# Expert stage: the down weights loaded from ScalarE's queue, gate and up weights left on SyncE's

## The reference, cut to what matters

```python
hn = rms_norm(h)                                  # 1040 x 1024
expert_idx, weights = top 2 of 8 experts in the best of 8 groups     # 64 experts
for every token t and each of its two experts e:
    g = hn[t] @ w_gate[e]                         # 1024 x 256
    u = hn[t] @ w_up[e]                           # 1024 x 256
    y = (silu(g) * u) @ w_down[e]                 # 256 x 1024
out[t] = h[t] + sum of weights * y
```

## Time and profile before

| | |
|---|---|
| time, median of 3 runs | 4101.42 us (4097.24 to 4104.04) |
| the profiled execution | 4109.06 us, span 4107.2 us |
| expert stage in the profile | 3415.4 us (first constant issued) to 4030.6 us (last scatter issued) |
| its assignment part | 3415.4 to 3473.7 us (first gate product) |
| its loop over the blocks | 3473.7 to 4030.6 us |
| loads of weights | 210 of 1024 KB, all on SyncE's queue |
| DMA queues over the span | q1 (SyncE's) 465.09 MB, q10 (ScalarE's) 112.70 MB, q0 (GpSimd's) 17.08 MB |

### The profile page before, as it was taken

The page is one execution under the profiler, slowest core; times in us unless marked ns, Lnnn a source line. Parts: engine busy times, 40 slices in busy tenths (PEclk is TensorE's granted clock), DMA queues, the critical chain, the costliest instruction groups (busy, mean ns, idle before and its releaser), DMA issues. The chain is left out here.

```text
span 4107.2 us, 80665 instructions
## 1 busy us (share of the span) xinstructions
PE 3411.6 (83%) x33244; PEld 2848.2 (69%) x33244; DVE 1585.4 (39%) x2597; ACT 995.8 (24%) x1970; POOL 345.2 (8%) x395
## 2 busy tenths in 40 slices
PE   7989988888859859998996799999959864978772
PEld 5867777788748759997986588888849643544441
DVE  3145643434245541115654345555444314111113
ACT  2022311122222021113443245444411011211111
POOL 0000000000000000000000223222100000222221
PEclk9999999999979979999998799999869965989986
DMA  3335455211344333324442311110033236999995
GB/s 103 95 101 190 148 180 182 88 49 43 113 148 139 125 94 93 93 74 151 162 142 92 97 27 52 48 38 23 23 108 119 87 95 248 414 417 409 410 410 197
DMA packets 325011, 598.26 MB, mean 146 GB/s; under 512 B 57427, under 2 KB 222140, under 8 KB 304728
## 3 DMA queue, kind: packets, MB, share of 16 engines
q1 hardware_dynamic: 275419, 465.09, 32.3%
q10 hardware_dynamic: 38436, 112.70, 7.8%
q0 software_dynamic: 10928, 17.08, 1.1%
HBM read 475.58 MB, written 139.97 MB: 150 GB/s over the span
## 5 line engine op out<-in xcount | busy, mean ns | idle before, releaser
L3052 PE MATMUL ex_bank_ps<-ex_w_gate_up_sb,ex_xT_sb 128*64 128x256 f32 x2240 | 290.9, 420 | 91.6 <-DMA ex_w_gate_up_sb<-in_w_up_e 89.9
L361 PE MATMUL in_bank_ps<-in_h_hi_sb,in_w_hi_sb 128*128 128x352 f32 (+4 forms) x968 | 332.6, 344 | 10.7 <-DVE in_w_lo_sb L316 10.7
L361 PE MATMUL in_bank_ps<-in_h_hi_sb,in_w_lo_sb 128*128 128x352 f32 (+4 forms) x968 | 332.6, 344 | 0.0
L361 PE MATMUL in_bank_ps<-in_h_lo_sb,in_w_hi_sb 128*128 128x352 f32 (+4 forms) x968 | 332.2, 343 | 0.0
L3052 PEld LDWEIGHTS ex_bank_ps<-ex_w_gate_up_sb,ex_xT_sb 128*64 128x64 f32 x2240 | 176.9, 152 | 214.6 <-issue 139.6
L1417 PE MATMUL mix_bank_ps<-mix_y_hi_sb,mix_wb_hi_sb 128*128 128x512 f32 (+2 forms) x480 | 171.5, 357 | 76.2 <-DVE mix_y_lo_sb L1498 54.0
L433 PE MATMUL qkv_tile_bank_ps<-in_h_hi_sb,qkv_tile_w_hi_sb 128*128 128x352 f32 (+1 forms) x576 | 188.9, 328 | 11.9 <-DVE qkv_tile_w_lo_sb L420 11.9
L361 PEld LDWEIGHTS in_bank_ps<-in_h_hi_sb,in_w_hi_sb 128*128 128x128 f32 (+1 forms) x968 | 181.2, 187 | 24.7 <-issue 11.4
L3240 DVE TENSOR_TENSOR ex_hidden_sb<-ex_silu_g_sb,ex_bank_ps 128x128 f32<-128x128 f32 x70 | 20.1, 288 | 453.3 <-ACT ex_silu_g_sb L3104 453.3
L361 PEld LDWEIGHTS in_bank_ps<-in_h_lo_sb,in_w_hi_sb 128*128 128x128 f32 (+1 forms) x968 | 181.3, 187 | 14.7
L361 PEld LDWEIGHTS in_bank_ps<-in_h_hi_sb,in_w_lo_sb 128*128 128x128 f32 (+1 forms) x968 | 181.3, 187 | 13.2
(11 more groups left out here) (460 smaller groups left out, 7714.4 us busy)
## 6 DMA issues: line engine op xcount, KB each, us to landing
ex_w_gate_up_sb<-in_w_gate_e SPq DMA_DIRECT2D x70, 1024.0 KB, 16.8
ex_w_gate_up_sb<-in_w_up_e SPq DMA_DIRECT2D x70, 1024.0 KB, 24.7
ex_w_down_sb<-in_w_down_e SPq DMA_DIRECT2D x70, 1024.0 KB, 25.0
in_w_sb<-in_w_in SPq DMA_DIRECT2D x45, 512.0 KB, 4.4
scr_p2T<-in_o_sb ACTq DMA_DIRECT2D x28, 520.0 KB, 3.0
qkv_x_sb<-scr_p2T SPq DMA_DIRECT2D x8, 1560.0 KB, 7.1
scr_p2T<-qkv_tile_o_sb ACTq DMA_DIRECT2D x24, 520.0 KB, 3.0
prep_tile_w_sb<-in_w_in SPq DMA_DIRECT2D x24, 512.0 KB
```

What stands on the lines that cost most here:

```text
L361: last = pe.matmul(bank[:width, 4 * s + n, 0:m], w_[:, s, k, 0:width], h_[:, k, a:a + m], start=(k == 0 and z == 0), stop=(k == KT - 1 and ...
L3052: last = t.matmul(bank[m * BT:(m + 1) * BT, GU_B + b % 2, 0:2 * P], xT[:, s, k, at:at + BT], wgu[:, ws, :, k, m * P:(m + 1) * P], start=(k ...
```

## The change

The down weights are loaded by ScalarE. Its first six loads stand ahead of its first wait, and each later pair of down loads stands behind the copies of the pair that frees the slots. SyncE issues gate and up alone and no longer waits for `y_done`. The last turn of ScalarE's loop is taken out of the loop, since there is nothing left to load behind it. No amount of data and no slot is changed.

```diff
@@ block.sync
-            def load_down(e, ws):
-                sp.dma_start(wd[:, ws, :, :],
-                             wd_d[ds(e, 1), :, :].rearrange("a (m p) d -> (a p) m d", m=M)).then_inc(d_ld[ws], 16)
-
             for b in range(TURN):
                 load_gate_up(b, b)
-                load_down(b, b)
             load_pairs(sp)
...
                 sp.wait_ge(gu_done, done(i, b))
                 load_gate_up(e, b % WS)
-
-                sp.wait_ge(y_done, done(i, b))
-                load_down(e, b % WS)
@@ block.scalar
             a.sem_inc(y_rdy, 2)
             c = Steps(a, ac)
+            def load_down(e, ws):
+                a.dma_start(wd[:, ws, :, :],
+                            wd_d[ds(e, 1), :, :].rearrange("a (m p) d -> (a p) m d", m=M)).then_inc(d_ld[ws], 16)
+
+            for b in range(TURN):
+                load_down(b, b)
             a.wait_ge(dv, at["shifted"])
...
             load_pairs(a)
-            with a.Fori(0, N_BLK // TURN) as i:
+            def compute(i, q):
...
+            with a.Fori(0, N_BLK // TURN - 1) as i:
                 for q in range(PT):
                     with in_use(a, i, q):
+                        compute(i, q)
+                    with in_use(a, i + 1, q):
                         for b in (2 * q, 2 * q + 1):
+                            load_down(a.value_load(table[0:1, ds((i + 1) * TURN + b, 1)], min_val=0, max_val=N_EXP - 1), b % WS)
+            for q in range(PT):
+                with in_use(a, N_BLK // TURN - 1, q):
+                    compute(N_BLK // TURN - 1, q)
```

More of the change, by code:

```diff
@@ L3095, in _ @@
             load_pairs(a)
-            with a.Fori(0, N_BLK // TURN) as i:
+            def compute(i, q):
+                for b in (2 * q, 2 * q + 1):
+                    s = b % 2
+                    a.wait_ge(gu_done, done(i, b, WS))
+                    a.wait_ge(h_rdy, done(i, b))
+                    a.activation(sg[:, s, :], bank[:, GU_B + s, 0:P], ACT.Silu).then_inc(sg_rdy, 1)
+                for b in (2 * q, 2 * q + 1):
+                    s = b % 2
+                    a.wait_ge(y_done, done(i, b, WS))
+                    a.wait_ge(y_free, done(i, b))
+                    a.activation(y[:, s, :], bank[:, Y_B + s, :], ACT.Copy).then_inc(y_rdy, 1)
+            with a.Fori(0, N_BLK // TURN - 1) as i:
                 for q in range(PT):
                     with in_use(a, i, q):
+                        compute(i, q)
+                    with in_use(a, i + 1, q):
                         for b in (2 * q, 2 * q + 1):
[L3100 to L3110, removed]
+                            load_down(a.value_load(table[0:1, ds((i + 1) * TURN + b, 1)], min_val=0, max_val=N_EXP - 1), b % WS)
+            for q in range(PT):
+                with in_use(a, N_BLK // TURN - 1, q):
+                    compute(N_BLK // TURN - 1, q)
         @block.vector
```

## The result

The changed kernel takes 4120.25 us (median of 5 runs, 4115.11 to 4124.24), the kernel before 4101.42 us: 1.0047 times as long, with a 95% interval of 1.0032 to 1.0061. Run again it was 1.0050 [1.0035, 1.0065], with medians of 4120.46 against 4104.22 us. By these ratios it is 19 to 20 us slower (by the medians 18.8 and 16.2); I had forecast +7.9 us.

A forecast was written before the change was run, and what follows sets the result against it. The prediction took transfers to bound the loop, and the constants' path to decide before it. Its terms, 8 − 0.7 − 1.9 + 2.5 = +7.9 us on 4101.4, gave 4109.3 us, with a range from 4099 to 4118.

The forecast's parts named there:

- GpSimd's rows: Gathers and scatters in the loop: a third queue costs each 1.3 us, covered by 4.9 us to spare a pair; cost 0.
- Six down loads beside the constants: Before the loop: constants take turns with ScalarE's first six down loads and land later, +8 us, between 0 and +12.3.
- First gather: Before the loop: the first weights start landing earlier, so the first gather may gain, −0.7 us, between 0 and −1.
- Start of the loop: First 10.2 us of loop loads: two blocks' gate and up are queued early and the transfer hole closes, −1.9 us.
- The long middle: The loop's 64 blocks: same bytes with the DMA engines full, so 0 us.
- the end: Behind the last loads: gate and up of block 69 become the last bytes, +2.5 us, between 0 and 2.7.
- ScalarE's own work: ScalarE in the loop: register loads and issues take some 2.6 us a pair, covered by 9.2 us; cost 0.
- A: Rival on the whole kernel: the constants slip through and there is no effect, −0.1 us, 4101.3 us; chance 0.16.
- B: Rival at the constants: engines serve whole loads in turn, so 12.3 us in place of 8, 4113.6 us; chance 0.13.
- C: Rival in the loop: ScalarE's down issues are held up and Silu comes late, +28 to +100 us, 4137 us; chance 0.08.
- D: Rival at the loop's end: two queues spread the rest evenly and constants slip through, −8.2 us, 4093.2 us; chance 0.06.

The follow-up runs named there:

- e1: The changed kernel, with ScalarE waiting for the seven constants before its first six down loads; 4109.79 us, 1.0015 of the kernel before.
- e2: The kernel before, with only its first six down loads moved to ScalarE's queue and all later ones on SyncE's; 4114.32 us, +0.29%.
- g1: The changed kernel, with GpSimd issuing the gather three pairs ahead behind its scatters, before their landing, and not waiting for that gather at once; 4117.91 us, 1.0042.
- g2: The changed kernel with both the constants waited for before ScalarE's first down loads and g1's early gather; 4106.28 us, 0.11% over the kernel before.
- h1: The changed kernel with w_down laid out for 8 KB rows on the down queue, gate and up products taking every second column; loop 570.6 us.
- g4: The changed kernel with each down load cut into two of half the columns, so rows are 2 KB instead of 4; loop 586.5 us.
- e3: The changed kernel, with GpSimd issuing the gather three pairs ahead behind its scatters, then waiting for that gather before going on; 4114.73 us, 1.0031.

## Why the prediction was wrong

The median, 4120.25 us, lies above the range, which ended at 4118, and the loss is more than twice the forecast's. The step that failed is that of GpSimd's rows, costed at 0: it cost 3 to 3.6 us of the 6 to 7 that the loop lost. The constants' term was right in kind and too small. Term by term:

*Six down loads beside the constants: +8 forecast, 10.4 measured* at the first reduce (15.2 behind the first constant against 4.8), 9 to 10 over the start, and 12 to 13 us in the times of e1 and e2. The mechanism, turns by packet, was right from 3418 us on: 367 packets against 365, and the row lengths move the price. The term was mis-sized. I had given the constants' own work 3.1 us on top of the turns as the upper end, and with 2 KB rows, where the turns cost half as much (4.1 us), 7.2 us are measured. So 2.2 us on top of the turns are there with 4 KB rows and 3.1 with 2 KB. With 8 KB rows 51 turns would take 16.4 us, more than the 15.3 us of all six loads, and 15.7 are measured, so nothing can be read there. The 2.5 us from 3413.5 to 3416 in which the constants' queue all but stood still are of this size; that they are the same time is argued. The forecast had no such gap.

*First gather: −0.7 forecast.* From the first reduce to the first gate product it is 53.1 us against 53.6 before, −0.4.

*Start of the loop: −1.9 forecast.* The share of the first ten us rose from 0.81 to 0.90 and not to 1.0: some −0.9 us of transfer.

*GpSimd's rows: cost 0 forecast.* This step failed. I took 8 turns of 0.159 us, 1.3 us for a gather or a scatter, against 4.9 us to spare. Measured: scatters +3.6 to 3.9 us, gathers +1.2 to +1.6 (8.1 before, 9.3 to 9.7 in e1, by the stretch). Three things were wrong in it. I held the 1.3 against the slack one at a time, where GpSimd's program puts gather, scatters and their landing in series. The scatters stand behind the gather on one queue: 24 rows an engine and not 8, and 24 x 0.159 = 3.8 us would fit; that is an estimate, and with one queue the scatters right behind a gather landed only 0.8 us later than the others (7.4 against 6.6 in the median, from 3560 us on). And the 4.9 us to spare are a mean over the 26 waits of 35 pairs; over all pairs it is 126.6 / 35 = 3.6 us. GpSimd's round grew by 3.5 us, from 12.9 to 16.4, and used up nearly all of that. TensorE's waits for gathered rows went from 5.6 to 99.7 us, and taking the chain away gave 3 to 3.6 us of the loop back (g1, g2).

*The long middle, 0, and the end, +2.5 forecast.* The transfers kept their rate, 413 GB/s. With GpSimd's chain gone the loop is 2.3 us (g2, the constants first) and 3.9 us (g1) over the kernel before. With the 0.9 us won at its start that leaves 3.2 to 4.8 us for the end, somewhat more than the +2.5, and the mechanism wasn't mine: the last gate and up products waited for no weight, since TensorE was behind the transfers and not on their heels.

*ScalarE's own work: 0 forecast.* Right: 0.389 us for an issue, and the 2.92 us before the table load stayed.

The rivals. A (no effect) is out: e2 alone costs 0.29%. B (whole loads in turn) gave 4113.6 us, nearer in time (its 12.3 us are 12.2 by their own sum). The even packet counts speak against it, and so does h1: with whole loads in turn the same loads in 8 KB rows would have cost the same, and they cost 5.3 us more. g4 doesn't tell, since its loads were of half the size too. That was also where the rule of the Trainium skill ("DMA: Bandwidth & Descriptors", section "Queues, rings and completion order") pointed, with 9 to 17 descriptors to a turn. Even counts alone, 367 to 365, don't say how many rows a turn has. But in every half microsecond from 3419.5 to 3425 us they differ by three at the most (49 and 48 from 3420 to 3420.5, 42 and 42 from 3422 to 3422.5), which fits single rows better; the order on one engine is not shown. C (ScalarE held up) didn't happen here and did in g4, whose down queue was the slower one; the 4.6 us an issue from which I let it decide left out the register loads, with which it is (9.2 − 1.8) / 2 = 3.7. D (faster) needed the end's tail to even out, and it didn't: the share falls over 20 us as before. The Trainium skill, "DMA: Bandwidth & Descriptors", section "Issuing engines are not separate DMA queues", says that a second issuing engine saves issue time only. The bandwidth agrees, 413 GB/s against 412; but the second queue wasn't free, because it took turns from the small transfers.

What stays open: some 2 to 5 us between the sum of the distances (15 to 17 us) and the 19 to 20 us by the ratios of the times, how the 2 to 4 us that g1 and g2 keep in the loop come about, what holds the constants up from 3413.5 to 3416, and why a scatter behind a gather pays so much more beside two queues than beside one.

## What to carry to other kernels

Before putting bulk loads on a second queue, look for the small transfers that something waits for: beside a busy queue each of their rows paid here for about one row of it, and the longer those rows, the more. Let such loads land before the bulk starts; here one wait was worth 13 us. When a wait is given slack, add up everything that stands in series in that engine's program, and read the length between two of its issues rather than one transfer. And try the new order on the old queue first: here the order was the gain (−0.16%) and the queue the loss.

## What the runs showed of the hardware that I had not expected

Beside two busy weight queues a scatter right behind a gather landed in 10.2 to 10.5 us and one ahead of it (e3) in 7.5, where beside one queue it was 6.6. With both queues freshly started, the small loads' queue all but stood still for 2.5 us, 24 packets against 212. Rows of 2 KB cost bandwidth in the loop, 392 against 413 GB/s. And a matmul that reads every second float32 column of its moving operand took 388 ns instead of 379.
